# A streaming encoder layer with a mixture of experts: the third expert pair's weights leave one wait and move behind another

## The reference

```
n2 = modulate(rmsnorm(x, norm2), sh2, sc2)
group  = top-1 of 4 groups, expert = top-2 of its 8 experts, per token
h   = silu(n2 @ w1[e]) * (n2 @ w3[e])          # w1, w3: 1024 x 256
x   = x + gt2 * sum_e gate[e] * (h @ w2[e])    # w2: 256 x 1024
y   = rmsnorm(x, final_norm)
```

## Time and profile before

| | |
|---|---|
| median of 3 runs | 722.2 us (720.06 to 724.82) |
| the profiled execution | 722.57 us |
| span in its trace | 720.7 us |
| PE busy | 619.6 us, 86% |
| DVE, ACT, POOL busy | 298.6, 199.6, 117.4 us |
| DMA | 191.00 MB, mean 265 GB/s over the span |
| SP's queue (q1) | 167.50 MB, 58.1% of the 16 DMA engines |

### The profile page before, as it was taken

One profiled execution on the slowest core, in us unless ns is written; L12 is line 12 of the kernel. 1 busy time (PEld: TensorE's weight loads), 2 busy tenths in 40 slices (PEclk: granted clock), 3 DMA queues, 4 the chain that ended last, 5 costly groups with the idle time before them and its releaser, 6 DMA issues. The chain is left out here.

```text
span 720.7 us, 8835 instructions
## 1 busy us (share of the span) xinstructions
PE 619.6 (86%) x3502; PEld 381.2 (53%) x3502; DVE 298.6 (41%) x410; ACT 199.6 (28%) x388; POOL 117.4 (16%) x137
## 2 busy tenths in 40 slices
PE   1689999996999989999999998799999988878720
PEld 0256788874766767767886775334444433223200
DVE  5899787246106567236585536200000000000017
ACT  5478623333134213002003044112222221111101
POOL 6894000020000321001000001202121111100003
PEclk9999999998999999999999999899999999999965
DMA  9933031287556556773530388899999999999742
GB/s 365 431 135 122 12 118 44 93 319 286 222 179 237 221 198 255 278 259 149 234 117 0 118 340 330 348 394 415 420 421 419 420 421 421 423 422 421 321 166 108
DMA packets 29272, 191.00 MB, mean 265 GB/s; under 512 B 5808, under 2 KB 6320, under 8 KB 13616
## 3 DMA queue, kind: packets, MB, share of 16 engines
q1 hardware_dynamic: 19488, 167.50, 58.1%
q0 software_dynamic: 8160, 18.89, 7.1%
q10 hardware_dynamic: 1584, 4.04, 1.4%
HBM read 184.49 MB, written 16.40 MB: 279 GB/s over the span
## 5 line engine op out<-in xcount | busy, mean ns | idle before, releaser
L503 PE MATMUL bank<-parts,parts 128*128 128x512 f32 x1080 | 260.5, 399 | 3.7 <-DVE working L1557 2.0
L503 PEld LDWEIGHTS bank<-parts,parts 128*128 128x128 f32 x1080 | 201.3, 189 | 64.0 <-issue 14.9
L847 PE MATMUL bank<-weights,working 128*64 128x512 f32 x352 | 84.8, 632 | 10.9 <-DMA weights<-in_p_up 9.6
L1727 DVE TENSOR_TENSOR working<-working,bank 128x256 f32<-128x256 f32 x16 | 6.7, 421 | 203.1 <-ACT working L1256 203.1
L847 PEld LDWEIGHTS bank<-weights,working 128*64 128x64 f32 x352 | 29.7, 145 | 63.8 <-issue 51.2
L1463 DVE TENSOR_TENSOR parts<-weights,parts 128x4096 fp32r<-128x4096 f32 (+1 forms) x10 | 40.0, 3999 | 39.9 <-ACT parts L1104 39.8
L875 PE MATMUL bank<-weights,working 128*64 128x512 f32 x176 | 40.2, 597 | 6.6 <-issue 4.3
L1883 POOL DMA_INDIRECT working<-n_rows,working x16 | 16.9, 1056 | 158.1 <-PE bank L826 137.4
L847 PE MATMUL bank<-working 128*64 128x512 f32 x160 | 37.4, 616 | 5.0 <-DMA working<-in_p_up 5.0
L1256 ACT ACTIVATE working<-bank 128x256 f32<-128x256 f32 x16 | 6.2, 385 | 114.3 <-PE bank L847 114.3
L1269 ACT ACTIVATE working<-bank,working 128x512 f32<-128x512 f32 x32 | 20.3, 684 | 58.7 <-PE bank L875 58.7
(11 more groups left out here) (281 smaller groups left out, 708.1 us busy)
## 6 DMA issues: line engine op xcount, KB each, us to landing
weights<-in_p_up SPq DMA_DIRECT2D x22, 2048.0 KB, 24.4
weights<-in_p_in SPq DMA_DIRECT2D x11, 2048.0 KB, 8.6
weights<-in_p_down SPq DMA_DIRECT2D x11, 2048.0 KB, 24.8
working<-in_p_up SPq DMA_DIRECT2D x8, 2048.0 KB, 33.5
working<-in_p_ada SPq DMA_DIRECT2D x12, 1024.0 KB, 6.0
working<-in_p_down SPq DMA_DIRECT2D x10, 1024.0 KB, 27.5
weights<-in_p_ada SPq DMA_DIRECT2D x4, 2048.0 KB, 19.0
weights<-in_p_ada SPq DMA_DIRECT2D x4, 1024.0 KB, 7.1
```

What stands on the lines that cost most here:

```text
L503: ins = mm(o[:, :], x[:, k, 128 * t:128 * t + 128], w[:, k, lo:lo + 512], start=k == 0 and n == 0, stop=k == kt - 1 and n == 2)
L847: ins = mm(ps[2 + u][64 * e:64 * e + 64, :], xgT[:, u, k, 64 * e:64 * e + 64], ups[slot][:, e, 512 * k:512 * k + 512], start=k == 0, stop= ...
```

## The change

In SP's list the wait for `n2_out` (L1000) is taken out, and the load of `downs[2][0]` changes places with the wait for `gathered0`, the landing of the first gather. So the two 1 MB loads into `wup2[:, 1]` follow on the gate row `("g2", 1, 1)` and on `n2_ssq` alone, and the 1 MB load of `downs[2][0]` now stands behind the first gather. Nothing is changed on other engines, and the loads move the same bytes.

```
@@ -997,15 +997,14 @@
 
             multiplied(sp, ("g2", 1, 1))
             sp.wait_ge(S["n2_ssq"], T)
-            sp.wait_ge(S["n2_out"], 16 * T)
             sp.dma_start(wup2[:, 1, FIRST], A["p_up"][2, :, 1, FIRST]).then_inc(S["up_in2"], 16)
             sp.dma_start(wup2[:, 1, SECOND], A["p_up"][2, :, 1, SECOND]).then_inc(S["up_late2"], 16)
             for g in range(4):
                 copied(sp, ("x2T", "P", g))
             for g in range(2):
                 copied(sp, ("x2T", "S", g))
+            sp.wait_ge(S["gathered0"], 16)
             sp.dma_start(downs[2][0], A["p_down"][2, :, 0, :]).then_inc(S["down_in2"], 16)
-            sp.wait_ge(S["gathered0"], 16)
             sp.dma_start(wup2[:, 0, FIRST], A["p_up"][2, :, 0, FIRST]).then_inc(S["up_in2"], 16)
             sp.dma_start(wup2[:, 0, SECOND], A["p_up"][2, :, 0, SECOND]).then_inc(S["up_late2"], 16)
             sp.wait_ge(S["records_ready"], 1)
```

## The result

The changed kernel takes 725.17 us (median of 20 runs, 723.45 to 728.2), the kernel before 721.68 us in the same rounds. The ratio is 1.0046, with a 95% interval of 1.0034 to 1.0058: 0.46% slower, about 3.3 us, where 1.4 us less was forecast. It lies within the 1% of the chances, but on the other side and outside the range (717.5 to 724.8). The profiled execution took 723.45 us, the least of the twenty, and its span is 721.7 us.

What follows compares the result with a forecast made beforehand. Weights through the DMA engines at 420 GB/s bound the expert stage. Later stores, a quicker gather and four loads behind it started pair 3's weights 1.4 us earlier: median 720.8 us, range 717.5 to 724.8.

Steps and rivals of the forecast that it cites:

- the 1% of the chances: Chances for the whole kernel's time: within 1% of before 0.92, faster by over 1% 0.04, slower by over 1% 0.04.
- The bound: Expert stage: it ends when the weights have come through, bytes over 420 GB/s; only DMA idle time before 474 us is winnable.
- Part 1, the landing of the stores: Removed wait in SP's queue: 2.10 MB more beside the stores, whose last landing moves from 450.3 to 452.8 us.
- The middle: Last store's landing put at 452.8 us, between 450.3 (served as before) and 455.3 us (drain and tail both move).
- rival (a): Stores served last, behind SP's weights: landing at 455.2 us, pair 3's weights start at 472.2, 1.0 us slower; chance 0.15.
- Part 2, the quicker gather: First gather, down weights moved behind it: takes 3.9 us instead of 7.8, landing at 457.6 us.
- is not moved: DVE's wait on the stores, met before L1701 started at 452.86 us, was claimed to be unaffected.
- The sum: Start of pair 3's weights after the first gather and four loads: 469.8 instead of 471.2 us, so 1.4 us won.
- The break-even of the prediction: First gather landing at 459.0 us: pair 3's weights then start as before, at 471.2 us.
- The release of pair 3's weights: PE's halfway signal in pair 0: load issued at 467.7 us at the latest, before the 468.5 us needed, so no bound.
- the 8.9 us from PE's start to the load: Pair 0 on PE: read before from 461.02 to 469.93 us, used to place pair 3's load after the change.
- the worst rival: First gather slow in itself, 7.8 us: pair 3's weights start at 473.7 us, 2.5 us slower; chance 0.1.

Runs made afterwards that it cites:

- e5_one_early: The half dose: the change, but one of pair 2's two early loads waits for the stores' landing and the other has no wait; 720.90 us, ratio 0.9996 against before.
- e3_all_behind: The kernel before with all of pair 2's loads (6.29 MB) behind the landing of the first gather; 726.37 us, ratio 1.0070.
- e7_behind_issue: `e4_two_stores` with the four loads waiting for the first gather's issue instead of its landing; 718.48 us, ratio 0.9964 against the kernel before.
- e9_three_early: `e7_behind_issue` with the down weights ahead of the wait for the first gather's issue; 722.70 us, ratio 1.0009 against the kernel before.
- e2_move_only: The kernel before with only the down weights moved behind the first gather, the wait for the stores kept; 721.22 us, ratio 0.9999.
- e4_two_stores: The change, but pair 2's two early loads wait for the first two of the three stores; 720.93 us, ratio 0.9993 against the kernel before.
- e6_two_stores_three: `e4_two_stores` with the down weights ahead of the first gather again; 721.38 us, ratio 0.9985 against the kernel before.

## Why the prediction was wrong

**The bound held.** The expert stage ends with the weights, and what the DMA engines move before t + 60 sets when; the flow afterwards is 420 GB/s in both profiles.

**Part 1, the landing of the stores, is the step that failed.** I set two ends, 450.3 and 455.3 us, and took "the middle, 452.8 us, since the packet counts show the stores neither served first nor shut out for good". On t this is 26.9, and the two profiles of the change have 28.5 and 28.7, nearer to the upper end of t + 29.4. The rival (a) put its decision at 454.2 us, t + 28.3; it was passed by 0.2 and 0.4 us, and (a)'s 1.0 us slower is close to what the bytes give. But it was not (a)'s mechanism: the stores were not served last. The middle was no reading of a row: with 2.10 MB beside them the stores share with weights from 442 to 450 us, about 70 to 80 packets of each queue in 2 us, but the stores' packets carry 0.24 MB where the weights' carry 0.58. A third of 420 GB/s for 1.57 MB, from 442 us on, is some 11 us, to about 453 us, and the last store landed at 453.65. That the stores would get the smaller part could be read from the earlier trace rows (3.6 KB a packet against 13), though not its size, since pair 2's 1 MB loads move 8 KB a packet (0.58 MB in 73). The half dose shows the slope, 2 us for each of the first two loads. (The Trainium skill, "DMA: Bandwidth & Descriptors", Queues, rings and completion order, has the turns by packet: from 442 us on the trace agrees, 71 packets of the stores and 73 of the weights from 444 to 446 us. In the prediction it was set aside for the late onset alone, and its sharing would have given the larger delay.)

**Part 2, the quicker gather, was right in its mechanism and too small in size.** It was to take 3.9 us; it took 3.8 where its issue lay as before (`e3_all_behind`, `e7_behind_issue`) and 4.7 and 4.8 us in the change. The missing 0.9 us is the issue, 2.46 us instead of 1.46, since the late stores now release DVE's wait and POOL's together. In all these profiles the first gather's issue, where it starts while DVE is in a product of the picks, ends 0.98 to 0.99 us behind that product. Before, it was the product on 480 elements, which ended 0.47 us into the issue (452.86 and 0.66 against 453.05 us); now it is the one on 1440, which ends 1.47 us into it. I had written that DVE's wait "is not moved". It was, by the same miss; even a landing at the forecast 452.8 us left it only 0.06 us.

**The sum.** Landing of the gather: forecast t + 31.7, measured t + 34.2 and 34.5, of which the stores are 1.7 us and the issue 0.9. The break-even of the prediction, a landing at 459.0 us, is t + 33.1: by its own formula the change had to come out 1.1 to 1.4 us slower, and the bytes give 1.3 and 1.9. The timed loss is 2.3 to 3.3 us; the difference is the offset left open above.

**The early PE.** The release of pair 3's weights was forecast at t + 41.8 at the latest and came at t + 41.8 and t + 40.7; it was no bound in the change, as argued. It was one in `e9_three_early` and in the kernel before, and the prediction missed why. This is PE's timeline before:

```profile
463.32 10.00 PE L847 MATMUL bank<-weights,working 128*64 128x512 f32 x32 [1.24 <-ACT working L1249]
```

PE had stood idle 2.19 us for the gather, and from 463.32 to 469.32 us its granted clock was 0.51. In the three profiles in which PE waited more than 2 us there (before, its repeat and `e9_three_early`) these 32 products take 9.9 to 10.0 us, in all others 7.1. So the 8.9 us from PE's start to the load were a reading at about half clock; in the change they are 6.0 us (461.04 to 467.01 us). Where PE doesn't run idle for the gather, the release thus comes 3 us earlier still, which no term of the prediction has. The down weights' later place and the later gathers cost nothing that shows: `e2_move_only` is the kernel before to 0.2%.

**The range** left out the measured time, by 0.4 us. Its upper end had the worst rival at 724.7 us, but not the rival together with the 1.5 us that a median can be off, which was only taken off the lower end.

## What to carry to other kernels

Where the DMA engines bound the stage, compare what two orders have moved by a common time; a hole that is filled counts nothing if a dependent small transfer is pushed into opening another. A small store or gather that others wait for should find no large loads ahead of it. If the queue ahead has run out by then, loads may be issued right behind it: that made 2.1 us here (`e7_behind_issue` against `e4_two_stores`), but with part of 3.15 MB still ahead, loads behind the issue slowed the gather by 2.0 us (`e9_three_early` against `e6_two_stores_three`). The loads ahead of the stores cost all that they were to bring. Look also at what the waiting engine's granted clock does: PE's idle time of over 2 us was followed by six microseconds at about half clock. When two queues share, estimate each one's part from bytes a packet in the trace, and take no middle between two ends.

## What the runs showed of the hardware

A store on ACT's queue issued behind a full queue of SP's moved next to nothing at first (one packet before 442 us, the first store issued at 438.04). It then took turns with it packet by packet: 70 and 68, 71 and 73, 81 and 79, 81 and 76 packets in the four windows of 2 us from 442 to 450. No run here has a store without weights ahead, so how much of the 4 us is the queue's and how much the store's own start is not shown; a load of SP's in empty queues took 1.3 us from its issue until it flowed.

Loads issued 1.7 us behind a gather's issue did not slow it where 2.10 MB ahead had been issued some 4 us before it (3.8 us with them, 3.9 in `e4_two_stores` without). Behind 3.15 MB the gather took 6.2 to 7.8 us with nothing behind its issue and 8.2 us with loads there. Behind 2.10 MB it took 3.9 to 5.2 us, the less the earlier these had been issued.

POOL's issue of an indirect DMA takes 0.99 us alone, and where it starts during a product of DVE it ended 0.99 us behind that product: 2.46 us in three profiles, with 1.47 us of the 1440-element product to go, 1.46 and 1.25 us with 0.47 and 0.27 us of the 480-element one to go (before and `e5_one_early`), and 1.11 us with the products held back. The second gather's issue, where it starts during such a product, ends 0.88 to 0.89 us behind it. (The Trainium skill, "SBUF — State Buffer", SBUF: two separate sides, says that DVE and GpSimd share a port pair which is an exclusive lock: a DVE operation with two SBUF inputs holds it for the whole instruction against a GpSimd operation that reads SBUF. The trace agrees with such a wait; the port itself is not seen in it.)
